# Experts in two kinds of blocks, 160 and 128 rows, with one long and one short place in a turn of the loop

## The reference

```
def swiglu(x, wg, wu, wd):
    return (jax.nn.silu(x @ wg) * (x @ wu)) @ wd
...
    eidx, gw = route(hf, w_router, router_bias)
    routed = routed_experts(hf, eidx, gw, w_e_gate, w_e_up, w_e_down, blk)
    shared = swiglu(hf, w_s_gate, w_s_up, w_s_down)
    return (routed + shared).astype(h.dtype).reshape(B, S, D)
```

## Time and profile before

| | |
|---|---|
| median of three runs | 2244.16 us |
| the profiled execution, its own time | 2246.8 us |
| its span, first to last instruction | 2245.0 us |
| mean granted clock of TensorE | 0.971 of full speed |
| busy: PE, DVE, ACT, POOL | 94%, 60%, 47%, 46% of the span |
| HBM read and written | 442.3 MB and 125.1 MB, 253 GB/s over the span |

### The profile page before, as it was taken

One profiled execution on the slowest core, in us unless ns is written; L12 is line 12 of the kernel. 1 busy time (PEld: TensorE's weight loads), 2 busy tenths in 40 slices (PEclk: granted clock), 3 DMA queues, 4 the chain that ended last, 5 costly groups with the idle time before them and its releaser, 6 DMA issues. The chain is left out here.

```text
span 2245.0 us, 42905 instructions
## 1 busy us (share of the span) xinstructions
PE 2102.4 (94%) x15302; PEld 1587.1 (71%) x15302; DVE 1342.1 (60%) x2337; ACT 1050.0 (47%) x1584; POOL 1031.8 (46%) x850
## 2 busy tenths in 40 slices
PE   7999889979799989999898979999999999999994
PEld 5777767757444448888687647777777777777773
DVE  4478757685576662111357546777777777767772
ACT  6321213266566661111243116666666666666662
POOL 2111223252577741111016614766676676767662
PEclk9999989979899999999999999999999999999997
DMA  6587811073655557982432268999999999999996
GB/s 224 158 260 254 265 63 38 27 225 116 204 170 164 162 171 248 296 275 89 136 146 93 98 230 306 330 339 342 333 333 339 343 331 336 332 339 340 336 327 158
DMA packets 178691, 520.62 MB, mean 232 GB/s; under 512 B 22908, under 2 KB 77355, under 8 KB 152143
## 3 DMA queue, kind: packets, MB, share of 16 engines
q1 hardware_dynamic: 130070, 355.43, 45.0%
q0 software_dynamic: 37520, 97.81, 17.0%
q10 hardware_dynamic: 10992, 66.02, 8.7%
HBM read 442.31 MB, written 125.08 MB: 253 GB/s over the span
## 5 line engine op out<-in xcount | busy, mean ns | idle before, releaser
L2728 DVE TENSOR_TENSOR w_gu_lo<-turned,w_gu_hi 128x2048 fp32r<-128x2048 f32 x132 | 302.7, 2294 | 146.1 <-ACT w_gu_hi L2650 146.1
L2650 ACT ACTIVATE w_gu_hi<-turned 128x2048 fp32r<-128x2048 f32 x132 | 253.9, 1924 | 38.7 <-PEq L1930 38.7
L627 PE MATMUL pP<-wring,hT_hi 128*128 128x512 f32 (+1 forms) x576 | 227.6, 395 | 19.9 <-DVE wring L553 12.5
L629 PE MATMUL pP<-wring,hT_lo 128*128 128x512 f32 (+1 forms) x576 | 222.5, 386 | 0.0
L628 PE MATMUL pP<-wring,hT_hi 128*128 128x512 f32 (+1 forms) x576 | 222.4, 386 | 0.0
L2577 PE MATMUL pG_e<-w_gu_hi,xT_hi 128*128 128x512 f32 x528 | 215.5, 408 | 0.0
L2577 PE MATMUL pG_e<-w_gu_lo,xT_hi 128*128 128x512 f32 x528 | 209.9, 398 | 0.0
L2577 PE MATMUL pG_e<-w_gu_hi,xT_lo 128*128 128x512 f32 x528 | 209.3, 396 | 0.0
L2504 POOL DMA_INDIRECT x_scratch<-turned,target x66 | 106.8, 1619 | 199.0 <-ACT turned L2691 199.0
L393 POOL TENSOR_TENSOR wring<-turned,wring 128x512 fp32r<-128x512 f32 (+1 forms) x43 | 71.1, 1679 | 229.1 <-ACT wring L427 228.8
L2490 POOL DMA_INDIRECT turned<-h_scratch,index x64 | 166.2, 2596 | 20.0 <-issue 20.0
(11 more groups left out here) (335 smaller groups left out, 5033.9 us busy)
## 6 DMA issues: line engine op xcount, KB each, us to landing
turned<-in_w_e_up SPq DMA_DIRECT2D x65, 1024.0 KB, 11.1
turned<-in_w_e_down SPq DMA_DIRECT2D x65, 1024.0 KB, 6.8
turned<-in_cache_sb_kv SPq DMA_DIRECT2D x256, 256.0 KB, 3.1
turned<-in_w_e_gate SPq DMA_DIRECT2D x64, 1024.0 KB, 7.1
out<-in_cache_win_kv ACTq DMA_DIRECT2D x8, 4094.0 KB
turned<-in_w_in ACTq DMA_DIRECT2D x56, 256.0 KB, 6.8
turned<-in_w_in SPq DMA_DIRECT2D x16, 512.0 KB, 7.8
out<-in_cache_win_kv ACTq DMA_DIRECT2D x8, 1022.0 KB
```

What stands on the lines that cost most here:

```text
L627: pe.matmul(pP[:m, i % 4, :w], hi, w_hi(u), start=(c == 0), stop=False)
L629: last = pe.matmul(pP[:m, i % 4, :w], lo, w_hi(u), start=False, stop=(c == KC - 1))
L2650: act.activation(ghi[:, r, k, :, :].rearrange("p c f -> p (c f)"), w[:, r, k, :], ACT.Copy).then_inc(ghi_ready, 1)
L2728: dve.tensor_tensor(glo[:, r, k, :, :].rearrange("p c f -> p (c f)"), w[:, r, k, :], ghi[:, r, k, :, :].rearrange("p c f -> p (c f)").bitc ...
```

## The change

- Blocks are of two kinds: long ones of 160 rows and short ones of 128. An expert has as many blocks as before; of these, as many are long as its rows need beyond 128 each, in steps of 32. All long blocks stand first in the list, then all short ones. The number of turns is the larger of half the blocks (rounded up) and the number of long blocks.
- A turn of the loop has a long place and a short place. The long place of turn i takes block i of the list, the short place block turns + i. A short block in a long place has an empty tail. The short place has no tail gather, no turn_tail, no gate_up_tail, no tail in turn_hidden, no down_tail, no y_tail and no tail scatter. The tail's buffers (tail, xT_tail, hid_tail) are single now.
- The order of a turn is written out. PE: gate_up_tail, turn_rows (short), gate_up (long), down (short of the turn before), turn_hidden (long), turn_tail and turn_rows (long of the next turn), gate_up (short), down (long), turn_hidden (short), down_tail. put of the long place now stands at the end of ACT's turn, put of the short place in its middle.
- SP: the down weights of the short place wait for their split (wlo_ready) instead of for the matmuls. POOL: the main scatter waits for y alone, the tail scatter for y_tail.
- The table is read in units of 32 rows, by five indirect DMAs instead of one; count_blocks gets more steps on DVE; NBLK is 128 instead of 116.

```
@@ -40,9 +40,10 @@
 DE = 256
 BLK = 160
 QT = 4
+TAIL = BLK - P
+UNITS = BLK // TAIL
 TURN = 2
-NBLK = -(-((T * TOPK + E * (BLK - 1)) // BLK) // TURN) * TURN
-SLOTS = NBLK * BLK
+NBLK = 128
 EPS = 1e-6
 BIG = 1e30
@@ -1993,20 +1998,20 @@
                 pool.wait_ge(where_ready, 1)
                 pool.wait_ge(mlo_ready, NP)
                 pool.wait_ge(scattered, 16 * NT * TOPK)
-                pool.indirect_dma_start(table, None, by_block, bass.IndirectOffsetOnAxis(ap=where[:NBLK, 0:1], axis=0)).then_inc(table_in, 16)
+                for q in range(UNITS):
+                    pool.indirect_dma_start(table[:, 2 * q * TAIL:2 * (q + 1) * TAIL], None, by_unit,
+                                            bass.IndirectOffsetOnAxis(ap=where[:NBLK, q:q + 1], axis=0)).then_inc(table_in, 16)
...
@@ -2251,25 +2256,45 @@
 
                 def count_blocks():
                     chain(dve.tensor_copy(count[:, :], pC))
+                    dve.memset(kinds[:, :], 0.0)
                     chain(dve.memset(nblk[:, :], 0.0))
                     for j in range(CAP):
                         chain(dve.scalar_tensor_tensor(nblk[:, :], count[:, :], float(j * BLK), nblk[:, :], ALU.is_gt, ALU.add))
-                    chain(dve.tensor_tensor_scan(end[:, :], ones[:, :E], nblk[:, :], 0.0, ALU.mult, ALU.add))
-                    past, kept, first, row, used = (eb[:, c:c + 1] for c in range(5))
-                    chain(dve.tensor_scalar(hit[:, :], end[:, :], number[:, 0:1], None, ALU.is_le))
+                    longs, none = kinds[:, :E], float(UNITS * EXTRA)
+                    chain(dve.scalar_tensor_tensor(count[:, :], nblk[:, :], -float(P), count[:, :], ALU.mult, ALU.add))
+                    for j in range(CAP):
+                        chain(dve.scalar_tensor_tensor(longs, count[:, :], float(j * TAIL), longs, ALU.is_gt, ALU.add))
+                    chain(dve.tensor_tensor(kinds[:, E:], nblk[:, :], longs, ALU.subtract))
+                    chain(dve.tensor_tensor_scan(end[:, :], ones[:, :2 * E], kinds[:, :], 0.0, ALU.mult, ALU.add))
+                    long_blocks, blocks = end[:, E - 1:E], end[:, 2 * E - 1:]
+                    chain(dve.tensor_scalar(turn_used[:, :], turn_first[:, :], blocks, None, ALU.is_lt))
+                    chain(dve.tensor_reduce(turns[:, :], turn_used[:, :], AX_X, ALU.add))
+                    chain(dve.tensor_tensor(turns[:, :], turns[:, :], long_blocks, ALU.max))
+                    dve.tensor_scalar(expert_row[0:1, NBLK:], turns[0:1, :], -2.0, None, ALU.add).then_inc(row_ready, 1)
+                    half, kept, odd, block_no, past, short, first, own, key, held, unit, used, rest = (eb[:, c:c + 1] for c in range(13))
+                    chain(dve.scalar_tensor_tensor(block_no, odd, turns[:, 0:1], half, ALU.mult, ALU.add))
+                    chain(dve.tensor_scalar(hit[:, :], end[:, :], block_no, None, ALU.is_le))
                     chain(dve.tensor_reduce(past, hit[:, :], AX_X, ALU.add))
-                    dve.tensor_scalar(kept, past, float(E - 1), None, ALU.min).then_inc(eb_ready, 1)
+                    chain(dve.tensor_scalar(short, past, float(E), None, ALU.is_ge))
+                    chain(dve.scalar_tensor_tensor(kept, short, -float(E), past, ALU.mult, ALU.add))
+                    dve.tensor_scalar(kept, kept, float(E - 1), None, ALU.min).then_inc(eb_ready, 1)
+                    dve.wait_ge(eb_ready, 1)
                     chain(dve.tensor_tensor(hit[:, :], hit[:, :], end[:, :], ALU.mult))
                     chain(dve.tensor_reduce(first, hit[:, :], AX_X, ALU.max))
-                    chain(dve.tensor_scalar(row, past, float(CAP), -float(EXTRA), ALU.mult, ALU.add))
-                    chain(dve.tensor_tensor(row, row, number[:, :], ALU.add))
-                    chain(dve.tensor_tensor(row, row, first, ALU.subtract))
-                    chain(dve.tensor_scalar(used, number[:, :], end[:, E - 1:E], None, ALU.is_lt))
-                    chain(dve.tensor_tensor(row, row, used, ALU.mult))
-                    dve.tensor_scalar(where[:, :], row, float(EXTRA), None, ALU.add).then_inc(where_ready, 1)
-                    chain(dve.tensor_scalar(turn_used[:, :], turn_first[:, :], end[:, E - 1:E], None, ALU.is_lt))
-                    chain(dve.tensor_reduce(turns[:, :], turn_used[:, :], AX_X, ALU.add))
-                    dve.tensor_scalar(expert_row[0:1, NBLK:], turns[0:1, :], -2.0, None, ALU.add).then_inc(row_ready, 1)
+                    chain(dve.tensor_tensor(own, block_no, first, ALU.subtract))
+                    chain(dve.tensor_scalar(key, kept, float(CAP * BLK), 1.0, ALU.mult, ALU.add))
+                    chain(dve.scalar_tensor_tensor(hit[:, :E], base[:, :], key, longs, ALU.is_equal, ALU.mult, accum_out=held))
+                    chain(dve.scalar_tensor_tensor(unit, held, float(UNITS), own, ALU.mult, ALU.subtract))
+                    chain(dve.tensor_tensor(unit, unit, short, ALU.mult))
+                    chain(dve.scalar_tensor_tensor(unit, own, float(UNITS), unit, ALU.mult, ALU.add))
+                    chain(dve.scalar_tensor_tensor(unit, kept, float(UNITS * CAP), unit, ALU.mult, ALU.add))
+                    chain(dve.tensor_scalar(unit, unit, none, None, ALU.subtract))
+                    chain(dve.tensor_scalar(used, block_no, blocks, None, ALU.is_lt))
+                    chain(dve.tensor_tensor(unit, unit, used, ALU.mult))
+                    chain(dve.scalar_tensor_tensor(rest, short, unit, unit, ALU.mult, ALU.subtract))
+                    for q in range(UNITS - 1):
+                        dve.tensor_scalar(where[:, q:q + 1], unit, none + q, None, ALU.add)
+                    dve.tensor_scalar(where[:, UNITS - 1:], rest, -1.0, none + UNITS - 1, ALU.mult, ALU.add).then_inc(where_ready, 1)
 
...
                 def load_gate_up(it, j):
                     e = expert(it, j)
                     if seen(it, j, 2):
-                        sp.wait_ge(gut_ready, it * U + (j - 1))
-                        sp.nop(nofuse=True)
+                        if j == LONG:
+                            sp.wait_ge(gut_ready, it)
+                            sp.nop(nofuse=True)
                         sp.wait_ge(glo_ready, it * (2 * U) + (2 * j - 2))
                     for k in range(2):
                         if seen(it, j, 2 - k):
-                            load(e, j % 2, k)
+                            load(e, j, k)
 
                 def load_down(it, j):
                     e = expert(it, j)
                     if seen(it, j, 2):
-                        sp.wait_ge(y_ready, it * U + (j - 1))
-                    load(e, j % 2, 2)
+                        if j == LONG:
+                            sp.wait_ge(y_ready, it * U - 1)
+                        else:
+                            sp.wait_ge(wlo_ready, it * U)
+                    load(e, j, 2)
 
                 def body(it):
-                    for j in range(U):
-                        if seen(it, j, 1):
-                            load_gate_up(it, j)
-                        if seen(it, j, 2):
-                            load_down(it, j - 1)
+                    if seen(it, LONG, 1):
+                        load_gate_up(it, LONG)
+                        load_down(it - 1, SHORT)
+                    load_gate_up(it, SHORT)
+                    if seen(it, LONG, 1):
+                        load_down(it, LONG)
                 body(0)
                 last = load_last(sp)
                 with sp.Fori(1, last + 1) as it:
                     body(it)
-                load_down(last, U - 1)
-                sp.wait_ge(y_out, last * (U * 32) + U * 32)
+                load_down(last, SHORT)
+                sp.wait_ge(y_out, last * 48 + 48)
                 sp.dma_start(o[1][:, 0], sc["x2"][S:T, :]).then_inc(copied, 16)
                 sp.dma_start(half_rows(o[0][0], 0), half_rows(sc["x2"], 0)).then_inc(copied, 16)
                 sp.wait_ge(copied, 48)
                 def gather(it, j):
-                    r = j % 2
-                    if seen(it, j, 2):
-                        pool.wait_ge(x_psum, it * (3 * U) + 3 * (j - 1))
-                    pool.tensor_copy(index[:, r, :], slot_info[:, bass.ds(it * U + j, 1), 0:2]).then_inc(index_ready, 1)
+                    pool.wait_ge(x_psum, it * 5 if j == SHORT else it * 5 - 2)
+                    pool.tensor_copy(index[:, j, :], slot_info[:, bass.ds(it * U + j, 1), 0:2]).then_inc(index_ready, 1)
                     pool.wait_ge(index_ready, it * U + (j - 1))
                     pool.nop(nofuse=True)
-                    pool.indirect_dma_start(rows[r], None, sc["h2"], bass.IndirectOffsetOnAxis(ap=index[:, r, 0:1], axis=0)).then_inc(rows_in[r], 16)
-                    pool.indirect_dma_start(tail[r], None, h2_quarters, bass.IndirectOffsetOnAxis(ap=index[:, r, 1:2], axis=0)).then_inc(rows_in[r], 16)
```

(100 more changed lines are left out.)

152 lines of the change are left out of this document (77 added, 75 removed).

## The result

The kernel after takes 2262.68 us (median of four runs, 2258.35 to 2267.82) against 2243.3 us (four runs) before on the same chip: ratio 1.0088 [1.0075, 1.0102], slower by 0.9%. The prediction was 2176 us.

A forecast was written before the change was run, and what follows sets the result against it. DMA engines and the scatter loop were taken to bound the turn at 24.5 us. 2246.8 - 61.4 (31 turns) - 6.8 (first two turns) + 2.5 (front) - 3.0 (end) = 2178.1, as median 2176 us; range 2130 to 2225.

The forecast's parts named there:

- 24.7 us, if landings stay: Scatter loop on the single y buffer: a new turn of 2.33 + 1.93 + 8.8 plus 2.33 + 9.3 us.
- long half: Scatter loop, long place: put to main scatter 2.33, to tail scatter 1.93, tail landing 8.8 us, before the next put.
- short half: Scatter loop, short place: put to main scatter 2.33, then its landing 9.3 us, before the next put.
- 24.5 us of a DMA bound: Turn taken for the loop, between DMA bounds 23.3 and 25.35 and next to the scatter loop's 24.7; saves 1.98 us each.
- slower, the same loop with longer landings: Rival on the scatter loop: turn passes 26.48 us once two landings sum to over 19.9 us; about 2300 us, chance 0.08.
- today's longest: Longest scatter landings in the earlier trace, 11.3 and 10.6 us; at these the turn would be 28.5 us.
- In-order ACT: Rival: short place's put waits for two landings ahead of ACT's splits; turns 25.4 to 26.3, 2203 to 2231 us, chance 0.13.
- PE's floor: PE's work per turn, 26.48 - 3.60 = 22.88 us; with the wait for the short weights' second split 23.06 us.
- Today the wait costs nothing: In the kernel before, put's wait for the scatter landing is free, because ACT has idle time ahead of the rows' split.
- The DMA bounds: Turn limits from the DMA engines: 25.35 us if all packet time is work, 23.3 us with weights at 429 GB/s.
- the first rival: PE stays the bound, the engines' fullness being perhaps elastic: turns of 23.06, 2130.9 us, up to about 2150; chance 0.25.
- Front and end: Five table reads instead of one cost +2.5 us (0 to 5.1); the short last place saves 3 us (0 to 5).

The follow-up runs named there:

- the late load: Changed kernel with the short place's down load waiting again for the matmuls (y_ready), not for its split: 2178.6 us, ratio 0.9719 to the kernel before.
- the best version: Changed kernel with a y buffer for each place, aim ahead of the gather on POOL, and the short down load late again: 2152.45 us, ratio 0.9573.
- two y in the kernel before: Kernel before the change with two y and two y_tail buffers, nothing else: 2249.96 us, ratio 0.9993.
- aim first: Changed kernel with the short down load late again and aim ahead of the gather on POOL, one y buffer: 2170.95 us, ratio 0.9623.

## Why the prediction was wrong

**Where it failed.** The sentence is: "The down load of the short place now waits for its own split, earlier than today, so nothing queued behind it is later." It looked at SP's queue and not at the 16 engines that this load shares with the scatters. From it followed the condition "24.7 us, if landings stay", and the one that counts, the tail scatter's, didn't stay. By its own terms: long half 2.33 + 1.93 + 8.8 = 13.1 forecast, 3.83 + 12.51 = 16.3 measured; short half 2.33 + 9.3 = 11.6 forecast, 11.2 measured. The difference of 2.8 us in each turn is the landing's +3.7, less 0.4 and 0.5 elsewhere. Undoing the one wait gives 2178.6 us, so the step is shown, not only argued: the early load prolongs the landing and the loop pays for it. How the load does it is not shown.

**Two numbers agree by luck.** The short half came out near its forecast for another reason: its scatter lands after 6.6 us and not 9.3, and put doesn't wait for it; POOL's way from the scatter over the gather pair to the target takes 9.3 us. And the 2178.6 us of the late load lie next to the forecast 2176, but no turn there is the forecast's 24.5 us of a DMA bound: the mean of 24.25 is made of turns of 23.0 to 23.5, PE's own time, and of others up to 28.0.

**The rival had it.** The case "slower, the same loop with longer landings" named the mechanism and the point from which it decides, two landings over 19.9 us; it had 0.08. In after they are 12.3 and, in the short place, 6.6, together 18.9, which by that rule would be 25.5 us a turn and not 27.5. The rule missed POOL: in the short half the scatter lands unnoticed, behind POOL's 9.3 us. The chance was too small because the landing was taken from the rows as a constant. Within the old loop it looked like one; the same two lines as the earlier trace rows, from 1400 to 2170 us:

```profile
DMA to landing us min/median/max: 8.7/9.3/9.9
...
DMA to landing us min/median/max: 8.1/8.8/9.6
```

The extremes in the earlier trace rows belong to the first and the last blocks, so "today's longest" was not a price of the steady loop. But the last four tail scatters, where the weights run out, landed after 4.6 to 5.0 us and those of the loop after 8.8: the difference was the sign that other transfers set the landing, and that moving them would move it.

**In-order ACT**, the rival in which a late put holds up PE, happened in part: PE waits for the hidden rows, 58.9 us, and for put to have emptied pY_e, 38.4 us, and these 97 us are nearly all that it idles (101 us). But they are how the loop's period reaches PE, not a bound of their own: with put freed of the other place's landing the turn became 25.1 us.

**PE's floor was right.** 22.88 of work and 23.06 with the second split's chain were forecast; the quick turns of the best version are 22.98, with PE busy for 22.87 of 23.00. The places (33 turns) and "Today the wait costs nothing" were right too, the latter shown by two y in the kernel before, but it was no reason to leave the wait out of what a moved load can cost.

**The DMA bounds were wrong in kind.** "The turn could not be shorter than 25.35 us" took the packets' time for work. Turns of 23.0 and 23.3 run at the same share of 1.03 to 1.04 as before's 1.02, with 370 against 336 GB/s. The elastic reading, the first rival's, is the right one; even the lower bound of 23.3, from 429 GB/s and today's scatters, lies over 22.98. The Trainium skill (HBM Reference, Specifications) puts a core streaming alone at about 425 GB/s. The whole turns shown here reach 372 at most. In the quick turns PE is the bound, as it would be by that rule; the changed kernel, at 316 GB/s, is held by a landing, of which a rate says nothing.

**Front and end.** The end gave 2.3 us, forecast 3. The front's forecast +2.5 came out as +0.8 on POOL's path: from the first read of the table to the first gather that uses it are 11.54 us (1283.48 to 1295.02, with four more reads up to 1.30 us apart) against 10.75 before (1286.76 to 1297.51). In the start of the loop it can't be told: that is 1335.0 and, in experiments with the same front, anywhere from 1332.0 to 1348.0.

**Still open.** Why, with the same distances between issues, a turn lands its scatters in 8.3 or in 11.8 us, and what switches from the one to the other. The early down load keeps nearly every turn slow, without it most are quick. Neither the burst of four loads nor the overlap with the short place's gate and up is the switch. In the kernel with the late load alone three longer turns (24.5, 25.3 and 27.3 us), after 15 of at most 23.5, begin with a tail scatter that leaves 1.3 us late, because POOL was late with the main one:

```profile
1797.64 1.62 POOL L2532 DMA_INDIRECT x_scratch<-turned,target  x1 [3.40 <-issue]
1799.57 2.99 POOL L2537 DMA_INDIRECT x_scratch<-turned,target  x1 [0.30 <-issue]
```

The quick turns have 2.07 us idle and 1.58 us of issue there. But in the kernel with aim first as well, the same thing at 1821.13 us leaves the turns around it at 23.3. So a late scatter may start a streak where the target comes behind the gathers; no experiment tested that.

## What to carry to other kernels

A transfer that is released earlier is an edit to every transfer that shares the DMA engines: look for a landing on which something waits in a loop with a single buffer, and price that loop with the landing of a fuller moment. A wait that costs nothing because its engine idles anyway can become the bound once a shorter turn takes the idle time away. The cures worked here in this order: first the load moved back (0.9719), then a second buffer for the output of the scatter together with its indices copied ahead of the gathers (0.9573). Either of these two alone on top of the late load gave nothing clear (0.9673 and 0.9623), and both without it 0.981.

## What the runs showed of the hardware

- A DMA share of about 1.0 is no bound here: the same share went with 336 GB/s (before), 372 (quick turns with the late down load) and 330 at 0.98 (slow turns of the same trace).
- The same scatter of 32 tail rows landed after 4.6 to 5.0 us at the end of the kernel before, after 8.8 in its loop, after 12.3 with one load of 1 MB issued 2.0 us ahead of it, behind three others, and no sooner with that load issued 1.7 us behind it. With the load 4.5 us behind it was 8.3 in most turns and up to 12.0 in others. Its own bytes were the same each time.
- Turns of two lengths, 23.3 and about 26.8 us, follow one another in streaks within one execution, both kinds at a granted clock of 1.00 in the turns shown.
- Indirect transfers hold up small work behind them on POOL: from the index copy over the issue of two gathers to the end of the target copy are 8.1 us (1738.13 to 1746.26), and put waited for that copy in each long place.
